# Up projections of a mixture of experts loaded in halves of 2 MB, experts in a fixed order, small pieces for the last

## The chip, the cores and the metric

The kernel runs on one core of one Trainium2 chip. The metric is the device time of one execution in microseconds. Engines: PE is TensorE, DVE is VectorE, ACT is ScalarE, POOL is GpSimd, SP is SyncE, which here issues the DMAs. PEld is PE's weight load.

## The reference

One layer of an encoder trunk for 256 tokens of 2048 channels, float32. A token-mixing sub-layer comes first: RMSNorm, modulation by `c`, an input projection, four branches with gates, an output projection and a residual. The change is in the second, the experts:

```python
pg = softmax(ht @ rg_w + rg_b); pg_top, g_idx = top_k(pg, 1)          # 1 group of 4
le = (ht @ re_w + re_b).reshape(t, 4, 8); le = le[:, g_idx]           # its 8 experts
pe_top, e_idx = top_k(softmax(le), 2); weights = pg_top * pe_top / sum(pe_top)
y[e] = (silu(x @ w1[e]) * (x @ w3[e])) @ w2[e]     # w1, w3: 2048 x 512, w2: 512 x 2048
x = x + gt2 * sum over the two experts of weights * y[e];  out = rmsnorm(x, final_g)
```

There are 32 experts, each of 12 MiB: w1 and w3 (the up projections) of 4 MiB each, w2 (the down projection) of 4 MiB.

## The kernel before

The mixing part runs until about 800 us. Its output x1 (2 x 128 tokens, in `r_h`) is split into three bfloat16 parts, `xparts`, whose sum is x1. The router sorts the 512 pairs of token and expert by expert and cuts each expert's pairs into windows of 64 (`NWIN`). Each window is a **pass**. The number of passes, `n_pass`, is 32 if no expert has more than 64 pairs, as here, and at most `MAXPASS`, 39. `etab` holds the expert of each pass, `otab` its offset, `ntab` the number of passes; SP, PE, ACT and DVE read them into registers once `table_ready` is set. A loop over 1 to 38 with a condition `p < end_p` does the middle passes; the last is written out.

One pass on PE: `gather` (line 886) multiplies columns of `xparts` (the weights of the matmul) by a 0/1 matrix, two halves of 48 matmuls. DVE's `modulated` makes `xe` of it, which is scaled and shifted. `turn` (895) transposes the hidden values of the pass before, `turn_windows` (918) its windows. `first` (954, `first_last` 979 in the last pass) is the up projection of this pass, 16 blocks of 128 channels in four chunks of four. `second` (908, `last_second` 1058) is the down projection of the pass before, `combine` (935) adds its result back into token order, and DVE's `add_moe` (1762) adds it to x1. Between them stand DVE's `window` (1733), `hidden` (1768), `save_output`, `output_low`, and ACT's `select`, `silu`, `copy_windows`, `round_output`, `copy_hidden`.

Weights lie in `ring` (slots 0 to 3, eight chunks of 1 MiB for up weights; slot 4 for half of w2) and `r_b` (the other half). SP issues all loads in one order: for pass p, chunk 0 of w1 and w3, half of w2 of the pass before, chunk 1, the other half, chunk 2, chunk 3. It waits before each for `w13_used` or `w2_used`, which PE raises at the end of a chunk. A partition reads four rows of w1, 8 KB that lie together, or two rows of w2, 16 KB:

```python
e1_v = exp_w1.rearrange("e (c p j) n -> e p c j n", c=4, p=P)
xparts_k = xparts[:, :, :, :].rearrange("p i t (c q j) -> p i t c j q", c=4, j=4)
```

So block k of `xe` holds every fourth channel, and `gather` reads its weights with 8 bytes between columns; the transposes of x1 (815) and of the modulation rows (681) read float32 with 16 bytes between columns, except the rows of the last vector of three, which are contiguous.

Ahead of the table: chunks 1 to 3 and w2 of expert 0 are issued while the output projection runs, chunk 0 into `r_m` after the logits, and chunk 0 of the next pass's expert once the table is there.

Of the kernel before, what the change touches and what calls it, by code (L numbers as in the profile page):

```python
# [18 lines left out]
P = 128  # L19
# [9 lines left out]
F = D // 4  # L29
# [41 lines left out]
N_KEEP = K_EPS + 1  # L71
# [3 lines left out]
def build(nc, x, ada_w, w_in, pool_w, pool_scale, branch_w, w_o, router_w, exp_w1, exp_w3, exp_w2, final_g,  # L75
          columns, router_b, gt1_bias, keep_consts, mix_consts, iota_const, out):
    with ExitStack() as ctx:
# [30 lines left out]
        x1_k = x1.rearrange("p t (c q j) -> p t c j q", c=4, j=4)  # L108
# [9 lines left out]
        pair_win = r_m[:, 0:256].rearrange("p (t m j) -> p t m j", t=TT, m=2)  # L118
# [15 lines left out]
        def first_chunk(m):  # L134

            return r_m[:, m * 2048:(m + 1) * 2048]
# [27 lines left out]
        xparts_k = xparts[:, :, :, :].rearrange("p i t (c q j) -> p i t c j q", c=4, j=4)  # L164
# [42 lines left out]
        ntab = sb("ntab", [1, 2], I32)  # L207
# [90 lines left out]
        w13_in = [sem(f"w13_in{i}") for i in range(CHUNKS)]  # L298
# [12 lines left out]
        first_in = [sem(f"first_in{m}") for m in range(2)]  # L311
# [32 lines left out]
        e1_v = exp_w1.rearrange("e (c p j) n -> e p c j n", c=4, p=P)  # L344
        e3_v = exp_w3.rearrange("e (c p j) n -> e p c j n", c=4, p=P)
# [38 lines left out]
        def _(sp):  # L384
# [89 lines left out]
            def load_w2(e, h):  # L474

                sp.dma_start((slot(4), r_b[:, :])[h].rearrange("p (f n) -> p f n", f=2),
                             e2_v[bass.ds(e, 1), :, 2 * h:2 * h + 2, :].rearrange("e p f n -> (e p) f n")
                             ).then_inc(w2_in[h], 16)
# [23 lines left out]
            for c in (1, 2):  # L502
                sp.wait_ge(g_used, 128 + 4 * (5 + c))
                load_w13(0, c)
            sp.wait_ge(wo_done, 8)
            load_w13(0, 3)
            sp.wait_ge(logitT_done, 2)
            for m, w in enumerate((e1_v, e3_v)):
                sp.dma_start(first_chunk(m).rearrange("p (k n) -> p k n", k=4),
                             w[0:1, :, 0, :, :].rearrange("e p j n -> (e p) j n")).then_inc(first_in[m], 16)  # L510
            sp.wait_ge(table_ready, 1)
            n_pass = sp.value_load(ntab[0:1, 0:1], min_val=NE, max_val=MAXPASS)
            second_e = sp.value_load(etab[0:1, 1:2], min_val=0, max_val=NE - 1)
            load_w13(second_e, 0)
            with sp.Fori(1, MAXPASS) as p:
                with sp.If(p < n_pass):
                    before = sp.value_load(etab[0:1, bass.ds(p - 1, 1)], min_val=0, max_val=NE - 1)
                    e = sp.value_load(etab[0:1, bass.ds(p, 1)], min_val=0, max_val=NE - 1)
                    with sp.If(p > 1):
                        sp.wait_ge(w13_used, 4 * p + 1)  # L520
                        load_w13(e, 0)
                        for c in (1, 2):
                            sp.wait_ge(w2_used, 4 * p + 2 * c)
                            load_w2(before, c - 1)
                            sp.wait_ge(w13_used, 4 * p + c + 1)
                            load_w13(e, c)
                    with sp.If(p < 2):
                        for c in (1, 2):
                            sp.wait_ge(w13_used, 4 * p + c + 1)
                            load_w13(e, c)  # L530
                    sp.wait_ge(w13_used, 4 * p + 4)
                    load_w13(e, 3)
            last_e = sp.value_load(etab[0:1, bass.ds(n_pass - 1, 1)], min_val=0, max_val=NE - 1)
# [1431 lines left out]
```

## Time and profile before

| | |
|---|---|
| time, median of 3 runs | 1783.74 us (1783.24 to 1787.66) |
| the profiled execution | 1783.57 us, of which the span is 1781.8 |
| PE busy | 1702.7 us, 96% of the span |
| DVE, ACT busy | 970.7 and 427.7 us |
| DMA | 641.95 MB, mean 360 GB/s |
| chain that ended last | PE 60%, DMA 35%, DVE 2% |
| up projections (line 954) | 1968 matmul records, 448.4 us |

Busy time of PE is modelled at its ends, so 96% doesn't say that PE is at its peak. The chain names, back from the last instruction, what released each step. The expert stage is the second half, from about 830 us. The DMA view counts packets; those under 512 B are the signals at the end of a transfer, one per DMA engine.

### The profile page before, as it was taken

How to read it: one execution, taken by the hardware profiler on the slowest of the kernel's cores; microseconds unless marked ns; L12 is line 12 of the kernel's file. 1: busy time of each engine (PE TensorE's matmuls, PEld its weight loads, DVE VectorE, ACT ScalarE, POOL GpSimd, SP SyncE). 2: the span in 40 equal slices, each digit the busy share in tenths (PEclk: the TensorE clock that was granted, in tenths of full speed). 3: DMA queues.
4: the chain of work that ended last, by engine and by line, in shares of the span. 5: the costliest groups of instructions: out<-in, count | busy, mean ns of one | idle time of the engine just before them, and what ended most of it. 6: DMA issues, size and time to landing. Idle time of an engine off the chain costs nothing.

```text
span 1781.8 us, 26191 instructions
## 1 busy us (share of the span) xinstructions
PE 1702.7 (96%) x10198; PEld 998.9 (56%) x10198; DVE 970.7 (54%) x1199; ACT 427.7 (24%) x534; POOL 0.9 (0%) x5
## 2 busy tenths in 40 slices
PE   4999999999999999999999999999999999999986
PEld 3888567777777776875444444444444444444442
DVE  5564959867778678566353443434343434343434
ACT  3001034433333233443121212121212121111111
POOL 0000000000000000000000000000000000000000
PEclk9999999999999999999999999999999999999998
DMA  9998538889879697835999999999999999999995
GB/s 369 387 385 323 189 142 336 334 311 352 331 287 361 259 367 317 308 131 211 414 423 425 423 425 423 425 423 425 424 425 424 424 424 425 423 425 424 425 424 241
DMA packets 128239, 641.95 MB, mean 360 GB/s; under 512 B 8003, under 2 KB 8131, under 8 KB 76099
## 3 DMA queue, kind: packets, MB, share of 16 engines
q1 hardware_dynamic: 127762, 639.18, 89.3%
q0 software_dynamic: 144, 1.70, 0.2%
q8 instruction: 31, 0.51, 0.1%
q10 hardware_dynamic: 290, 0.46, 0.1%
q14 instruction: 12, 0.10, 0.0%
HBM read 639.21 MB, written 2.10 MB: 360 GB/s over the span
## 4 chain that ended last, share of the span: by engine, by line
PE 60%; DMA 35%; DVE 2%; SPq 1%; issue 1%; DVEq 0%; ACT 0%
DMA ring<-in_exp_w 33%; PE ps L954 11%; PE ps L699 7%; PE ps L701 7%; PE ps L700 7%; PE ps L604 6%; PE ps L661 5%; PE ps L908 3%; PE ps L617 3%; DMA ring<-in_ada_w 2%; PE ps L772 2%; PE ps L773 2%; PE ps L774 2%; PE ps L886 1%; DVE r_m L1380 1%
## 5 line engine op out<-in xcount | busy, mean ns | idle before, releaser
L954 PE MATMUL ps<-ring 128*64 128x512 f32 x1968 | 448.4, 597 | 24.5 <-DMA ring<-in_exp_w 24.5
L954 PEld LDWEIGHTS ps<-ring 128*64 128x64 f32 x1968 | 145.9, 136 | 287.3 <-issue 287.2
L1762 DVE SCALAR_TENSOR_TENSOR r_h<-ps,stat,r_h 128x1024 f32<-128x1024 f32 x124 | 153.4, 1279 | 141.8 <-PE ps L935 141.8
L1721 DVE TENSOR_TENSOR r_c<-ps,scale 128x512 f32<-128x512 f32 x64 | 44.3, 692 | 305.4 <-PE ps L886 298.5
L700 PE MATMUL ps<-g_lo,h_hi 128*128 128x512 f32 x512 | 199.3, 389 | 0.0
L699 PE MATMUL ps<-mix_hi,h_hi 128*128 128x512 f32 x384 | 156.5, 408 | 0.0
L1155 ACT ACTIVATE mix_hi<-ring 128x1024 fp32r<-128x1024 f32 x96 | 101.5, 1061 | 222.3 <-PE ps L701 222.3
L701 PE MATMUL ps<-mix_hi,h_lo 128*128 128x512 f32 x384 | 149.6, 390 | 0.0
L1294 ACT ACTIVATE y_hi<-ring 128x512 fp32r<-128x512 f32 x62 | 38.1, 631 | 444.1 <-DVE ring L1749 444.1
L604 PE MATMUL ps<-r_h,ring 128*128 128x256 f32 x640 | 141.1, 383 | 1.3 <-ACT r_h L1106 1.3
L1472 DVE SCALAR_TENSOR_TENSOR r_m<-ring,col,r_m 128x2048 f32<-128x2048 f32 x53 | 124.4, 2347 | 31.8 <-DMA ring<-in_ada_w 31.8
L1486 DVE TENSOR_TENSOR g_lo<-ring,mix_hi 128x1024 fp32r<-128x1024 f32 x96 | 115.0, 1223 | 33.7 <-ACT mix_hi L1155 32.3
L604 PEld LDWEIGHTS ps<-r_h,ring 128*128 128x128 f32 x640 | 122.7, 192 | 18.3 <-issue 1.4
L886 PEld LDWEIGHTS ps<-r_c,xparts 128*128 128x128 bf16 x3024 | 106.0, 118 | 40.5 <-issue 39.6
L886 PE MATMUL ps<-r_c,xparts 128*128 128x64 bf16 x3024 | 112.8, 198 | 3.4 <-issue 3.4
L908 PE MATMUL ps<-r_b,r_c 128*64 128x512 f32 x496 | 113.2, 598 | 0.0
L908 PE MATMUL ps<-ring,r_c 128*64 128x512 f32 x496 | 111.7, 592 | 0.0
L700 PEld LDWEIGHTS ps<-g_lo,h_hi 128*128 128x128 f32 x512 | 96.2, 188 | 22.7 <-issue 3.6
L661 PE MATMUL ps<-ring,r_b 128*128 128x512 f32 x208 | 91.8, 592 | 0.0
L699 PEld LDWEIGHTS ps<-mix_hi,h_hi 128*128 128x128 f32 x384 | 72.2, 188 | 18.1 <-issue 2.9
L1749 DVE TENSOR_TENSOR ring<-ps,r_m 128x512 f32<-128x512 f32 x62 | 40.0, 687 | 74.8 <-PE ps L908 74.8
L701 PEld LDWEIGHTS ps<-mix_hi,h_lo 128*128 128x128 f32 x384 | 72.0, 188 | 15.2
(280 smaller groups left out, 1768.8 us busy)
## 6 DMA issues: line engine op xcount, KB each, us to landing
ring<-in_exp_w SPq DMA_DIRECT2D x254, 1024.0 KB, 23.2
ring<-in_ada_w SPq DMA_DIRECT2D x78, 1024.0 KB, 8.3
ring<-in_w_in SPq DMA_DIRECT2D x36, 2048.0 KB, 10.1
ring<-in_exp_w SPq DMA_DIRECT2D x32, 2048.0 KB, 24.3
r_b<-in_exp_w SPq DMA_DIRECT2D x32, 2048.0 KB, 25.3
ring<-in_w_in SPq DMA_DIRECT2D x20, 1024.0 KB, 14.2
r_b<-in_ada_w SPq DMA_DIRECT2D x18, 1024.0 KB, 9.9
ring<-in_w_o SPq DMA_DIRECT2D x8, 2048.0 KB, 8.3
```

Of the source, the lines that this page charges most:

```text
L604: last = mm(u[:, f, :], head_w(i)[:, kk, f * P:(f + 1) * P], hT[:, k, :], start=(begin and f % 2 == 0), stop=end, skip_group_check=True)
L661: last = mm(ps[:, y_bank(n) + t, :], lhs(k, t), rhs(k), start=(k == 0), stop=(k == kts - 1))
L699: mm(ps[:, b + t, :], h, hi[:, cols], start=(k == 0), stop=False)
L700: mm(ps[:, b + t, :], h, lo[:, cols], start=False, stop=False)
L701: last = mm(ps[:, b + t, :], h_lo[:, k, t * P:(t + 1) * P], hi[:, cols], start=False, stop=(k == KT - 1))
L886: last = mm(gat[:, kk, :], xparts_k[:, i, t, k // 4, k % 4, :], chosen[:, t, 0:NWIN], start=(t == 0 and i == 0), stop=(t == TT - 1 and i = ...
L908: last = mm(ps[side * NWIN:(side + 1) * NWIN, 4 + b, :], hid[:, f, :], chunk(CHUNKS + f)[:, q * MIX:(q + 1) * MIX], start=(f == 0), stop=( ...
L954: last = mm(ps[m * NWIN:(m + 1) * NWIN, 2, :], xe[:, k, :], w[:, kk * F:(kk + 1) * F], start=(k == 0), stop=(k == KT - 1))
L1155: A(g_hi[x % 4], slot(q % W_SLOTS)[:, (x % 4) * 1024:(x % 4 + 1) * 1024], ACT.Copy).then_inc(g_hi_done, 1)
L1472: ins = V.scalar_tensor_tensor(out=acc, in0=w, scalar=ccol[:, k:k + 1], in1=acc, op0=ALU.mult, op1=ALU.add)
L1486: V.tensor_tensor(g_lo[:, q, (x % 4) * 1024:(x % 4 + 1) * 1024], slot(q)[:, (x % 4) * 1024:(x % 4 + 1) * 1024], g_hi[x % 4].bitcast(F32), ...
L1762: V.scalar_tensor_tensor(out=x1n, in0=ps[:, (6, 4)[t]:(6, 4)[t] + 2, :].rearrange("p b n -> p (b n)"), scalar=tok_w[:, t:t + 1], in1=x1n, ...
```

## The change

- A load of up weights is 2 MiB: half of w1 or half of w3, with eight rows (16 KB) together per partition. Channel blocks are ordered 2 x 128 x 8 instead of 4 x 128 x 4, for x1, `xparts`, the modulation columns and the router's weights too. There are four pieces per pass, in four slots; `w13_used` rises twice per pass.
- SP's order is now: two pieces (the first halves), both halves of w2 of the pass before, two pieces. PE's order is first half, the whole of `second`, `gather` for the next, second half with two `combine` after its first and two after its second four blocks.
- Experts have a fixed order. Passes 0 to 15 are the first windows of experts 0 to 15, without the table. Then follow the further windows of any expert, at most 7 passes, from the table (none here), then experts 16 to 31. PE, ACT, DVE and SP each have three loops instead of one, and the condition stands only in the middle one. `ntab` gets two more entries.
- Expert 1's first piece is loaded ahead of the router, into slot 3; expert 0's last piece goes to `r_m[:, 0:4096]`.
- The last expert's second halves come in four pieces of 1 MiB, its w2 in four pieces of 1 MiB, each awaited by itself.
- DVE does both `save_output` before the next `modulated`. In the tail, the order of `last_combine` and `last_add` is by token half, `last_mean(0)` comes before the fourth add, and the squares follow that order.

```diff
+K_LATE = K_EPS + 1
+N_KEEP = K_LATE + 1
+EARLY = NE // 2
...
-        x1_k = x1.rearrange("p t (c q j) -> p t c j q", c=4, j=4)
+        x1_k = x1.rearrange("p t (c q j) -> p t c j q", c=2, j=8)
...
-        pair_win = r_m[:, 0:256].rearrange("p (t m j) -> p t m j", t=TT, m=2)
+        pair_win = r_m[:, 10048:10304].rearrange("p (t m j) -> p t m j", t=TT, m=2)
...
-        def first_chunk(m):
-
-            return r_m[:, m * 2048:(m + 1) * 2048]
+        def w13_slot(p, i):
+
+            if p == 0:
+                return r_m[:, 0:4096] if i == 3 else slot(i)
+            return slot((i + 3) % 4)
+
+        def w2_slot(h):
+
+            return slot(4) if h == 0 else r_b[:, :]
...
-        xparts_k = xparts[:, :, :, :].rearrange("p i t (c q j) -> p i t c j q", c=4, j=4)
+        xparts_k = xparts[:, :, :, :].rearrange("p i t (c q j) -> p i t c j q", c=2, j=8)
...
-        e1_v = exp_w1.rearrange("e (c p j) n -> e p c j n", c=4, p=P)
-        e3_v = exp_w3.rearrange("e (c p j) n -> e p c j n", c=4, p=P)
+        e1_v = exp_w1.rearrange("e (c p j) n -> e p c j n", c=2, p=P)
+        e3_v = exp_w3.rearrange("e (c p j) n -> e p c j n", c=2, p=P)
...
-            def load_w13(e, c):
-
-                for m, w in enumerate((e1_v, e3_v)):
-                    sp.dma_start(chunk(2 * c + m).rearrange("p (k n) -> p k n", k=4),
-                                 w[bass.ds(e, 1), :, c, :, :].rearrange("e p j n -> (e p) j n")
-                                 ).then_inc(w13_in[2 * c + m], 16)
-
+            def load_w13(p, e, i, landed):
+
+                w, c = (e1_v, e3_v)[i % 2], i // 2
+                sp.dma_start(w13_slot(p, i).rearrange("p (k n) -> p k n", k=8),
+                             w[bass.ds(e, 1), :, c, :, :].rearrange("e p j n -> (e p) j n")).then_inc(landed[i], 16)
+
+            for i in range(3):
+                sp.wait_ge(g_used, 128 + 4 * (5 + i))
+                load_w13(0, 0, i, first_in)
             sp.wait_ge(wo_done, 8)
-            load_w13(0, 3)
+            load_w13(1, 1, 0, w13_in)
             sp.wait_ge(logitT_done, 2)
+            load_w13(0, 0, 3, first_in)
+            sp.wait_ge(w13_used, 2 + 1)
+            load_w13(1, 1, 1, w13_in)
+            load_w13(1, 1, 2, w13_in)
+            sp.wait_ge(w13_used, 2 + 2)
+            load_w13(1, 1, 3, w13_in)
+
+            def load_front(p, e, prior):
+
+                sp.wait_ge(w13_used, 2 * p + 1)
+                for i in range(2):
+                    load_w13(1, e, i, w13_in)
+                for h in range(2):
+                    sp.wait_ge(w2_used, 4 * p + 2 * h + 2)
+                    load_w2(prior, h)
+                sp.wait_ge(w13_used, 2 * p + 2)
+
+            def load_pass(p, e, prior):
+
+                load_front(p, e, prior)
+                for i in range(2, 4):
+                    load_w13(1, e, i, w13_in)
+
+            with sp.Fori(2, EARLY) as p:
+                load_pass(p, p, p - 1)
             sp.wait_ge(table_ready, 1)
             n_pass = sp.value_load(ntab[0:1, 0:1], min_val=NE, max_val=MAXPASS)
+            end_p = sp.value_load(ntab[0:1, 1:2], min_val=NE - 1, max_val=MAXPASS - 1)
+            more = sp.value_load(ntab[0:1, 2:3], min_val=0, max_val=MAXPASS - NE)
+            more_end = sp.value_load(ntab[0:1, 3:4], min_val=EARLY, max_val=EARLY + MAXPASS - NE)
+            with sp.Fori(EARLY, EARLY + MAXPASS - NE) as p:
+                with sp.If(p < more_end):
+                    prior = sp.value_load(etab[0:1, bass.ds(p - 1, 1)], min_val=0, max_val=NE - 1)
                     e = sp.value_load(etab[0:1, bass.ds(p, 1)], min_val=0, max_val=NE - 1)
+                    load_pass(p, e, prior)
+            with sp.Fori(EARLY, NE - 1) as e:
+                p = e + more
+                prior = sp.value_load(etab[0:1, bass.ds(p - 1, 1)], min_val=0, max_val=NE - 1)
+                load_pass(p, e, prior)
+            load_front(end_p, NE - 1, NE - 2)
+            for j in range(2):
+                for m, w in enumerate((e1_v, e3_v)):
+                    sp.dma_start(w13_slot(1, 2 + m)[:, j * 2048:(j + 1) * 2048].rearrange("p (k n) -> p k n", k=4),
+                                 w[NE - 1, :, 1, 4 * j:4 * j + 4, :]).then_inc(last13_in[2 * j + m], 16)
+            for f in range(FT):
+                sp.wait_ge(w2_used, 4 * n_pass + f + 1)
+                sp.dma_start(chunk(CHUNKS + f), e2_v[NE - 1, :, f, :]).then_inc(last2_in[f], 16)
...
-                pe.wait_ge(x1_ready, m + 1)
+                pe.wait_ge(x1_ready, 4 * t + 2 * (n // 2) + 2)
...
+            def first_half(p, c, kks):
+
+                for kk in kks:
+                    k = 8 * c + kk
                     for m in range(2):
+                        last = mm(ps[m * NWIN:(m + 1) * NWIN, 2, :], xe[:, k, :],
+                                  w13_slot(p, 2 * c + m)[:, kk * F:(kk + 1) * F],
+                                  start=(k == 0), stop=(k == KT - 1))
+                return last
+
+            def gather_next(p):
+
+                pe.wait_ge(sel_ready, p + 2)
+                pe.wait_ge(xe_ready, 2 * p + 2)
+                gather(0, sel_e)
+
+            def first_pass():
+
+                for c in range(2):
+                    pe.wait_ge(xe_ready, c + 1)
                     for m in range(2):
+                        pe.wait_ge(first_in[2 * c + m], 16)
+                    first_half(0, c, range(8)).then_inc(w13_used, 1)
+                    if c == 0:
+                        gather_next(0)
+
+            def whole_pass(p, is_last=False):
+
+                pe.wait_ge(xe_ready, 2 * p + 1)
+                gather(1, sel_e)
+                turn(p)
+                turn_windows(p)
+                for m in range(2):
+                    pe.wait_ge(w13_in[m], 16 * p)
+                first_half(1, 0, range(8)).then_inc(w13_used, 1)
+                second(p, 0, 4)
+                if not is_last:
+                    gather_next(p)
+                pe.wait_ge(xe_ready, 2 * p + 2)
+                for m in range(2):
+                    if is_last:
+                        pe.wait_ge(last13_in[m], 16)
+                    else:
+                        pe.wait_ge(w13_in[2 + m], 16 * p)
+                first_half(1, 1, range(4))
+                for i in range(2):
+                    combine(p, i)
+                if is_last:
+                    for m in range(2):
+                        pe.wait_ge(last13_in[2 + m], 16)
+                first_half(1, 1, range(4, 8)).then_inc(w13_used, 1)
+                for i in range(2, 4):
+                    combine(p, i)
...
+            mm(ps[0:32, 1, 226:227], ones[0:32, 0:32], ct[:, 1, 0:1], start=True, stop=True).then_inc(start_done, 1)
...
+            first_pass()
+
+            with pe.Fori(1, EARLY) as p:
+                whole_pass(p)
...
+            with pe.Fori(EARLY, EARLY + MAXPASS - NE) as p:
+                with pe.If(p < more_end):
+                    whole_pass(p)
+            with pe.Fori(EARLY, NE - 1) as e:
+                whole_pass(e + more)
+            whole_pass(end_p, is_last=True)
...
-                    pe.wait_ge(w2_in[f // 2], 16 * n_pass)
+                    pe.wait_ge(last2_in[f], 16)
...
             last_combine(0, 0, 6)
+            last_combine(0, 1, 0)
             last_combine(1, 0, 2)
-            last_combine(0, 1, 0)
             pe.wait_ge(tail_added, 1)
             last_combine(1, 1, 6)
...
-            step(V.tensor_scalar(ntab[:, 1:2], ps[0:1, 1, 384:385], -1.0, None, ALU.add))
+            for i, less in ((1, 1), (2, NE), (3, NE - EARLY)):
+                step(V.tensor_scalar(ntab[:, i:i + 1], ps[0:1, 1, 384:385], -float(less), None, ALU.add))
...
+            def whole_pass(p):
+
+                off = v.value_load(otab[0:1, bass.ds(p, 1)], min_val=0, max_val=PAIRS)
+                window(p, off)
+                modulated(p, 1)
+                hidden(p)
+                for b in range(2):
+                    save_output(p, b)
+                modulated(p + 1, 0)
+                for b in range(2):
+                    output_low(p, b)
+                for i in range(4):
+                    add_moe(p, i)
+
...
-            last_add(1, 0, 2, 2)
-            last_add(0, 1, 0, 3)
-            last_add(1, 1, 6, 4)
-            v.wait_ge(fg_in, 16)
+            last_add(0, 1, 0, 2)
+            last_add(1, 0, 2, 3)
 
             def last_mean(t):
 
-                v.wait_ge(sq_done, 6 + 3 + t)
+                v.wait_ge(sq_done, 6 + 2 + 2 * t)
...
             last_mean(0)
+            last_add(1, 1, 6, 4)
+            v.wait_ge(fg_in, 16)
             scaled(0, 0)
+            scaled(0, 1)
             last_mean(1)
-            scaled(0, 1)
             scaled(1, 0)
             scaled(1, 1)
```

## Rows read from the trace of the kernel before

**Rows 1.** the page's 40 slices of the span, GB/s of the DMA engines

```profile
GB/s 369 387 385 323 189 142 336 334 311 352 331 287 361 259 367 317 308 131 211 414 423 425 423 425 423 425 423 425 424 425 424 424 424 425 423 425 424 425 424 241
```

**Rows 2.** busy time of PE, weight load, DVE, ACT, POOL, then clock, DMA share, GB/s

```profile
850.00:1700.00 850.00, 816.35 (x6218) 358.56 (x6216) 346.25 (x523) 156.33 (x235) 0.00 (x0) 1.00 1.01 423
```

**Rows 3.** the chain, expert stage: start us, us, what

```profile
1336.48 25.27 DMA ring<-in_exp_w
...
1366.15 25.26 DMA ring<-in_exp_w
```

**Rows 4.** the chain, passes 0 and 1 and two starts after them

```profile
829.68 7.02 PE ps L954 x32
...
838.41 7.02 PE ps L954 x32
...
847.92 3.58 PE ps L954 x16
851.51 3.43 PE ps L908 x16
...
858.37 1.72 PE ps L886 x48
...
863.68 3.43 PE ps L954 x16
...
871.82 0.68 PE ps L935 x4
...
876.02 3.58 PE ps L954 x16
...
904.11 3.58 PE ps L954 x16
```

**Rows 5.** DMA view of 830:842 us (40 slots), then 842:870 us

```profile
GB/s 0 0 0 0 0 273 164 55 191 437 437 410 437 437 437 437 410 437 437 437 437 437 437 219 27 27 410 27 0 246 410 437 382 437 437 410 410 437 382 437
DMA packets 481, 3.56 MB, mean 297 GB/s; under 512 B 47, under 2 KB 47, under 8 KB 47
...
DMA packets 1390, 11.25 MB, mean 402 GB/s; under 512 B 153, under 2 KB 153, under 8 KB 153
```

**Rows 6.** DMA view of 10:60 us, then 1041:1700 us

```profile
DMA packets 9729, 19.35 MB, mean 387 GB/s; under 512 B 289, under 2 KB 289, under 8 KB 9728
...
DMA packets 31978, 279.43 MB, mean 424 GB/s; under 512 B 3552, under 2 KB 3552, under 8 KB 3552
```

**Rows 7.** the chain, the last two passes

```profile
1692.47 25.27 DMA ring<-in_exp_w
...
1717.88 3.65 PE ps L954 x16
...
1722.67 3.39 issue
...
1729.51 4.14 PE ps L979 x16
...
1757.56 8.78 PE ps L1058 x32
```

**Rows 8.** busy time in five us of the tail, as rows 2

```profile
1755.00:1760.00 5.00, 3.41 (x14) 1.59 (x16) 0.42 (x1) 2.75 (x5) 0.00 (x0) 0.79 0.53 221
```

**Rows 9.** weight loads of lines 681 (two windows), 886, 852: ns min/median/max

```profile
L681 PEld LDWEIGHTS ps<-keep,r_m x16: 197/204/212, 472.6 to 482.7; 128*128 128x128 f32 x16
...
L681 PEld LDWEIGHTS ps<-keep,r_m x16: 138/139/141, 589.3 to 599.3; 128*128 128x128 f32 x16
...
L886 PEld LDWEIGHTS ps<-r_c,xparts x3024: 110/118/134, 827.9 to 1727.9; 128*128 128x128 bf16 x189
...
L852 PEld LDWEIGHTS ps<-xparts,r_c x8: 95/98/98, 813.4 to 821.7; 128*128 128x128 bf16 x8
```

**Rows 10.** the timeline, PE at line 681, strided and contiguous

```profile
472.78 0.63 PE L681 MATMUL ps<-keep,r_m 128*128 128x128 f32 x4
...
589.49 0.60 PE L681 MATMUL ps<-keep,r_m 128*128 128x128 f32 x4
```

More of the change, by code:

```diff
@@ L70 @@
 K_EPS = K_W + 3 * MAXWIN
-N_KEEP = K_EPS + 1
+K_LATE = K_EPS + 1
+N_KEEP = K_LATE + 1
+EARLY = NE // 2
 N_MIXC = 1024 * 3 + 256
@@ L937, in combine @@
                 last.then_inc(comb_done, 1)
-            def first(p, with_second):
-                for c in range(4):
-                    if c % 2 == 0:
-                        pe.wait_ge(xe_ready, 2 * p + c // 2 + 1)
+            def first_half(p, c, kks):
+                for kk in kks:
+                    k = 8 * c + kk
                     for m in range(2):
-                        if not with_second and c == 0:
-                            pe.wait_ge(first_in[m], 16)
-                        elif c == 0:
-                            pe.wait_ge(w13_in[m], 16 * p)
-                        else:
-                            pe.wait_ge(w13_in[2 * c + m], 16 * p + 16)
-                    for kk in range(4):
-                        k = 4 * c + kk
-                        for m in range(2):
-                            w = first_chunk(m) if c == 0 and not with_second else chunk(2 * c + m)
-                            last = mm(ps[m * NWIN:(m + 1) * NWIN, 2, :], xe[:, k, :], w[:, kk * F:(kk + 1) * F],
-                                      start=(k == 0), stop=(k == KT - 1))
-                    last.then_inc(w13_used, 1)
-                    if with_second and c == 0:
-                        second(p, 0, 2)
-                    if c == 1:
-                        pe.wait_ge(sel_ready, p + 2)
-                        pe.wait_ge(xe_ready, 2 * p + 2)
-                        gather(0, sel_e)
-                    if c == 1 and with_second:
-                        second(p, 2, 4)
-                    if with_second and c >= 2:
-                        for i in range(2):
-                            combine(p, 2 * (c - 2) + i)
@@ L969, in first_last @@
-            def first_last(p):
-                for c in range(4):
-                    if c % 2 == 0:
-                        pe.wait_ge(xe_ready, 2 * p + c // 2 + 1)
-                    for m in range(2):
-                        pe.wait_ge(w13_in[2 * c + m], 16 * p + (16 if c else 0))
-                    for kk in range(4):
-                        k = 4 * c + kk
-                        for m in range(2):
-                            last = mm(ps[m * NWIN:(m + 1) * NWIN, 2, :], xe[:, k, :],
-                                      chunk(2 * c + m)[:, kk * F:(kk + 1) * F],
-                                      start=(k == 0), stop=(k == KT - 1))
-                    last.then_inc(w13_used, 1)
-                    if c < 2:
-                        second(p, 2 * c, 2 * c + 2)
-                    if c == 2:
-                        for i in range(4):
-                            combine(p, i)
@@ L990, in _ @@
+            pe.sem_inc(w13_used, 2)
             pe.sem_inc(w2_used, 8)
```

148 lines of the change are left out of this document (59 added, 89 removed).

## Prediction, made before the changed kernel was run

> **What bounds the kernel now.** I read the page's slices first, then the busy time by stage, then the chain of waits, then the DMA view. The slices show 414 to 425 GB/s in all but the last slice of the expert stage, and 131 and 211 in the two before it, where the router runs [rows 1]. From 850 to 1700 us the DMA share is 1.01, while PE is busy 816 of 850 us [rows 2]: both look full, so the chain must decide. In its middle it repeats one link: 25.3 us from the issue of an expert's weights to their landing, one piece of up projection on PE, and the next issue. From issue to issue is 29.67 us [rows 3]. An expert is 12 MiB (8 of up, 4 of down projection), 12.58 MB, so 29.67 us is 424 GB/s: the queue sets the pace. PE alone is quicker: early on, while it lives on preloaded weights, one pass takes 904.11 - 876.02 = 28.09 us [rows 4]. PE thus has 1.6 us to spare per pass; the queue has nothing. Only three things can move the end: when the queue gets its bytes after the router, what a byte costs, and the PE chain behind the last landings.
>
> **The queue's start.** The line w13_used is what the loads wait for. Before: 12 MiB of expert 0 lie ready at the router, and the first 2 MiB of the next expert wait for the table. GB/s by slots of 0.3 us show data from about 832.7, a gap from 836.9 to 838.7, then data again; the piece that let the second load go ended at 829.68 + 7.02 = 836.70, so an idle queue needs 2.0 us from release to data [rows 4, 5]. In 830 to 842 and 842 to 870 us it moved 3.56 and 11.25 MB [rows 5]; taking off 13 us at 424 GB/s (5.51 MB) leaves 9.30 MB by 857.0, with the 12 MiB about 20.8 MiB.
> After: expert 1 is known without the table, so 14 MiB lie ready. Releases now come in halves. The first half of pass 0 ends at 836.70: 4 MiB flow from 838.7 to 848.5. Its second half ends at 838.41 + 7.02 = 845.43: 2 MiB, until 853.4. The next release is the first half of pass 1, now 7.0 us long from 847.92, so 854.9, data at 856.9: the queue is dry for 3.5 us. At 856.9 it has 20.0 MiB. That is 0.8 MiB or **+2.0 us** behind before: preloading gives 2 MiB, and coarse release takes back more.
> From there, does it stay full? Pass 1 by the rows: down projection of 7.0 us until 861.9, gather 1.7, then 3.6 + 1.1 + 3.5 until 871.9, data at 873.9; the queue has work until 876.5. First half of pass 2 ends 876.0 + 7.0, data at 885.0, queue until 886.3. These margins of 2.6 and 1.3 us are thin, but grow by over 1.2 us per pass. In the steady state a half is released 12.3 + 7.0 + 2.0 us after the previous landing, against a pass of over 29 us, so 6 to 8 us are spare. I cost it at nothing; without that margin it would cost what is missing, once per pass.
>
> **What a byte costs.** Up weights come in rows of 16 KiB instead of 8 (eight rows of w1 behind one another), down weights had 16 already. Two rows give the cost of a packet: at 2 KB packets the saturated queue does 9729 packets, 19.35 MB in 50 us; in the expert stage 31978 packets, 279.43 MB in 659 us [rows 6]. Without the small packets (289 and 3552) that is 16 x 50 us / 9440 = 84.7 ns per packet of 2050 B, and 16 x 659 / 28426 = 370.9 ns per 9830 B. The line through both is 0.0368 ns per byte and 9.3 ns per packet. A pass has 1280 data packets, 80 per engine; after, 768, 48 per engine: 32 x 9.3 = 0.30 us off 29.67, so 29.37. From 21 MiB to the 368 that are through with pass 30 are 28.9 passes: **-8.7 us**. Bounds: nothing, if a packet over 8 KiB costs twice, and 12 us, if the intercept were 13 ns. I take 8.7, since the mix already holds 16 KiB packets.
> The Trainium skill ("DMA: Bandwidth & Descriptors", section "Why small descriptors are slow (HBM only)") speaks of a fixed overhead of about 3 cycles per packet, and holds that packing is only worth it up to 256 B. An estimate from that page, at its 850 MHz, is 3.5 ns per packet, so 3.3 us over the stage instead of 8.7, a total near 1782.4. The rows differ from it: they give 9.3 ns.
>
> **The stretch behind the last landings.** The last up piece of pass 30 landed at 1692.47 + 25.27 = 1717.74 before [rows 7]; by the two terms it lands at 1711.0. Before, PE then does one piece of 3.7 us and combines; then all is idle for 3.39 us ("issue" [rows 7]), where the loop of up to 38 runs through eight empty iterations. Pass 31 starts at 1729.51, 11.8 us after the landing. After, the two halves' worth is larger: 863.68 to 876.02, the same work from the second-last piece on, is 12.34 us [rows 4]: **+0.6 us**, coarser by 4.5 and without 3.9 of stall. The seven empty iterations that now stand in the middle cost some 3 us on each engine at pass 16 (3.39 x 7/8); the queue's 6 us of margin cover them, and PE regains them at 1.3 us per pass. Without that cover they cost 3.
> From pass 31 on: 14.0 for half and down projection, 3.6 + 1.1 + 3.5 to the last half's end at 22.2, 4.2 to the window (871.82 to 876.02 in the rows of a pass, DVE's adds in front of it), about 1 to the hidden product, so 27.5 instead of 1757.56 - 1729.51 = 28.05 [rows 7]: **-0.5 us**. The pieces of 1 MiB land about when that ends (8 MiB behind the first half's landing, 20 us), so they don't bind. The last down projection takes 8.78 us instead of 7.0, with a granted clock of 0.79 where it begins, so part of it at 1.2 GHz, after PE had waited for the hidden product [rows 7, 8]; PE waits there after the change too, and I leave it. Four adds, four scalings and two means on DVE are reordered, not fewer: nothing, plus or minus 0.5.
>
> **What else is added.** One 1-column matmul, one DVE operation of some 0.1 us ahead of the pass table, two behind it: nothing to 0.3 us, I take nothing, since PE still has gather parts to do. Waits for two x1 chunks instead of one: DVE is ahead of the transposes there. The order of DVE's modulated and save_output: both end before the combine that waits for them.
> Every gather reads its weights from xparts with 16 bytes between columns, not 8. What rows show of strides: float32 weights took 139 ns to load when contiguous and 204 when 16 bytes apart, yet four such transposes took 0.60 and 0.63 us; bfloat16 took 98 contiguous and 118 at 8 bytes [rows 9, 10]. No row has bfloat16 at 16 bytes. Below: nothing. Above: the 65 ns of float32 in place of the 20, all exposed, 96 x 45 ns = 4.3 us per pass. I take nothing, because the float32 row with one element in 16 bytes lengthened the load by a third and the sequence by only 10 ns each.
>
> **Sum.** -8.7 + 2.0 + 0.6 - 0.5 = -6.6. The profiled execution took 1783.57 us (span 1781.8), 0.2 under the median of 1783.74; so 1777.0, a span of 1775.2, 0.37% less.
>
> **Rivals.**
> *Row length is worth little* (0.20): the packet cost is by bytes above 8 KiB, and passes stay at 29.6. For: down weights with 16 KiB already in the mix, and the total stays under 425. Against: the fit. Then 1777.0 + 8.7 = 1785.7.
> *PE becomes the bound* (0.15), the slower side: gather's weight loads at 16 bytes. A gather has 48 matmuls in 1.72 us, 36 ns each [rows 4]; if each takes twice that (the bound above is 45 more), 96 of them add 3.4 us, a pass is 31.5, and pass 31 starts at 876 + 29 x 31.5 + 3 = 1792.5, so the total is 1783.6 - 0.5 + 63.0 = 1846. It decides from passes of 29.6 us on, so from 16 ns more per matmul. The Trainium skill ("SBUF — State Buffer", the note on cachelines) wants at least two hits in a 16-byte line for full bandwidth: 8 bytes apart has two, 16 has one. The float32 rows agree in kind, by 65 ns.
> *The queue runs dry early or at pass 16* (0.07): margins of 1.3 us are missed in several passes, 3 to 8 us, 1780 to 1785 and a bit over.
> *More is won* (0.06): intercept near 13 ns, or the clock stays up in the tail, 1770 to 1774.
> The forecast itself has 0.52, by itself 1772 to 1782.
>
> **Range and chances.** 1770 to 1790 leaves out the PE-bound rival and little else. 0.3% (5.4 us) is what can be told from no change. Faster than 1778.4: four fifths of the forecast's 0.52 and the 0.06, 0.48. Within: the rest of the forecast, the row-length rival, half the dry queue, 0.34. Slower: 0.18.
>
> **What would show it.** Landing to landing in the middle: 29.4 right, 29.67 wrong for the row term; over 30 with a DMA share under 1 means PE bounds. Gather of 48 at 1.7 us right, 3 wrong. The DMA rate has a hole near 853 to 857 and none at pass 16. The stall of 3.4 before the last pass is gone, and pass 31's first matmul is near 1723.4, the last down projection 27.5 later. The prediction fails if any of the first three fails; each alone is larger than the margin to 0.3%.

## The result: slower, with TensorE full where the queue had been

The changed kernel took 1821.19 us (median of 4 runs, 1818.2 to 1824.83), the one before 1783.96 beside it on the same chip: a ratio of 1.0206, interval 1.0192 to 1.022. The forecast was 1777.0 with a range to 1790, so both the time and the sign were wrong. The profiled execution took 1820.09 us, with a span of 1818.0. One of the eleven executions of the second kernel with packed parts (below) took 3566.03 us, twice the others, and is left out of its ratio.

The same views after, the page's slices first, with GB/s in 40 slices of the span:

```profile
GB/s 370 387 373 305 185 162 351 334 291 362 335 300 319 288 361 299 301 194 140 414 421 414 418 419 415 420 413 422 399 364 423 413 423 412 422 414 423 413 421 186
```

The busy time of PE, weight load, DVE, ACT and POOL in the expert stage, then clock, DMA share and GB/s:

```profile
850.00:1700.00 850.00, 843.78 (x5988) 408.27 (x5986) 326.15 (x497) 117.09 (x198) 0.00 (x0) 0.99 0.99 411
```

And one pass of the chain (start us, us, what):

```profile
912.07 3.02 PE ps L913 x48
...
915.87 7.02 PE ps L971 x32
922.89 6.87 PE ps L935 x32
929.76 3.02 PE ps L913 x48
932.77 3.58 PE ps L971 x16
936.36 1.12 PE ps L962 x8
937.48 3.58 PE ps L971 x16
941.07 1.12 PE ps L962 x8
942.19 3.02 PE ps L913 x48
945.21 0.56 PE ps L922 x4
945.77 0.22 PE ps L945 x2
```

Before, this chain repeated one 25.3 us transfer per expert [rows 3]; now it is PE from end to end, with no transfer and no other engine in it. The next pass starts at 945.99, so a pass is 30.12 us instead of 29.67. PE went from 816 to 844 of 850 us, and the queue from 423 to 411 GB/s [rows 2]: the slices no longer stand at one level but swing, most of them between 412 and 423. Two pieces of the pass stand out: the gathers (L913, which was L886) take 3.02 us for 48 matmuls where they took 1.72 [rows 4]. Their weight loads (ns min/median/max) show why:

```profile
L913 PEld LDWEIGHTS ps<-r_c,xparts x3024: 142/166/176, 831.0 to 1765.9; 128*128 128x128 bf16 x189
```

A load takes 166 ns instead of 118 [rows 9], and a matmul of the group 63 ns instead of 36 (a 48th of its time). 96 gather matmuls per pass at 27 ns more are 2.6 us.

PE also stops once in the middle, where the loop over extra passes makes seven turns that do nothing. That is the other sizeable piece in the changed kernel's chain:

```profile
1302.51 1.12 PE ps L962 x8
1303.63 6.22 issue
1309.85 3.10 PE ps L913 x48
```

and the tail, from the first matmul of pass 31:

```profile
1766.94 7.02 PE ps L971 x32
...
1794.07 8.65 PE ps L1089 x32
```

Pass 31 starts at 1766.94, not at the predicted 1723.4. What follows it takes 51.1 us, where the forecast had 51.8. So the loss lies ahead of pass 31: 6.4 of the 43.5 us have gone by the second half of pass 0, which begins at 844.84 instead of 838.41 [rows 4], and the passes behind it add the rest.

### The profile page after: what moved, and what is told of

It is laid out like the page before. It is cut to its first block, busy times and chain, and to the rows that moved or that the text cites. A ratio compares the mean times of both kernels' runs of the same rounds, so it can differ in the third digit from the quotient of the medians.

```text
span 1818.0 us, 25263 instructions
## 1 busy us (share of the span) xinstructions
PE 1768.8 (97%) x10200; PEld 1070.2 (59%) x10200; DVE 966.9 (53%) x1202; ACT 388.0 (21%) x503; POOL 0.8 (0%) x5
## 4 chain that ended last, share of the span: by engine, by line
PE 93%; DMA 3%; DVE 2%; SPq 1%; issue 1%; ACTq 0%; DVEq 0%; ACT 0%
PE ps L971 25%; PE ps L935 12%; PE ps L913 10%; PE ps L726 6%; PE ps L728 6%; PE ps L727 6%; PE ps L631 6%; PE ps L688 5%; PE ps L962 4%; PE ps L644 3%; DMA ring<-in_ada_w 3%; PE ps L799 2%; PE ps L801 2%; PE ps L800 2%; DVE r_m L1421 1%; PE ps L922 1%
## 5 line engine op out<-in xcount | busy, mean ns | idle before, releaser
L971 PE MATMUL ps<-ring 128*64 128x512 f32 x2032 | 461.5, 598 | 0.0
L971 PEld LDWEIGHTS ps<-ring 128*64 128x64 f32 x2032 | 138.8, 137 | 257.6 <-issue 256.3
L913 PEld LDWEIGHTS ps<-r_c,xparts 128*128 128x128 bf16 x3024 | 187.7, 168 | 43.6 <-issue 42.4
L913 PE MATMUL ps<-r_c,xparts 128*128 128x64 bf16 x3024 | 194.5, 226 | 6.5 <-issue 6.2
L1314 ACT ACTIVATE r_m<-ps 128x512 f32<-128x512 f32 x32 | 19.1, 597 | 297.1 <-PE ps L971 297.1
```

Of the source, the lines that this page charges most:

```text
L913: last = mm(gat[:, kk, :], xparts_k[:, i, t, k // 8, k % 8, :], chosen[:, t, 0:NWIN], start=(t == 0 and i == 0), stop=(t == TT - 1 and i = ...
L971: last = mm(ps[m * NWIN:(m + 1) * NWIN, 2, :], xe[:, k, :], w13_slot(p, 2 * c + m)[:, kk * F:(kk + 1) * F], start=(k == 0), stop=(k == KT ...
```

## The experiments

The theory after the result: the 16 bytes between the gather's weight columns make PE the bound. The rivals: 2 MB pieces that are released late, or the new order of the waits, hold PE back; or the stall at pass 16 does it.

**The gather alone set back.** The changed kernel with the gather's view as before, so 8 bytes between columns. It takes other channels of each token than the reference; all other work is the same. Here and in the versions with other strides, the gather for the first half of pass 0 (line 1032), which is not shown, gets the same edit.

```diff
-        xparts_k = xparts[...].rearrange("p i t (c q j) -> p i t c j q", c=2, j=8)
+        xparts_k = xparts[...].rearrange("p i t (c q j) -> p i t c j q", c=4, j=4)
...
-    last = mm(gat[:, kk, :], xparts_k[:, i, t, k // 8, k % 8, :], ...
+    last = mm(gat[:, kk, :], xparts_k[:, i, t, k // 4, k % 4, :], ...
...
```

> The changed kernel, only that gather reads its weights with 8 bytes between columns as before (so it takes the wrong channels of x1 for each block; the routing doesn't depend on it). Theory 'stride': 16 bytes between bfloat16 columns made each gather matmul 63 ns instead of 36 and PE the bound. Then gathers of 48 go back to 1.7 us, PE alone needs 28.1 us or less per pass, the queue is the bound again with 29.4 us from landing to landing, and the time is 1776 to 1781. Rival 'halves': releasing weights in halves and running the whole down projection in one go makes PE or the queue wait by itself. Then the time stays above 1790 though the gathers are short. If the rows of 16 KB save nothing, passes are 29.67 and the time is 1784 to 1790.

Measured: 1781.13 us, ratio to before 0.998 (0.997 to 0.999), just over the expected 1776 to 1781. 40 us come back with this edit alone, while the late releases, the new order and the stall are all still there, so none of them makes the loss by itself. The weight loads, and the chain late in its expert stage:

```profile
L913 PEld LDWEIGHTS ps<-r_c,xparts x2592: 110/118/134, 903.5 to 1684.3; 128*128 128x128 bf16 x200
```

```profile
1665.34 20.27 DMA ring<-in_exp_w
...
1694.72 20.26 DMA ring<-in_exp_w
```

The queue is the bound again, with 29.38 us from issue to issue.

**The gather alone changed.** The kernel before, with the gather at 16 bytes and nothing else (so here too other channels).

```diff
-        xparts_k = xparts[...].rearrange("p i t (c q j) -> p i t c j q", c=4, j=4)
+        xparts_k = xparts[...].rearrange("p i t (c q j) -> p i t c j q", c=2, j=8)
...
```

> The kernel before, only that gather reads its weights with 16 bytes between columns (wrong channels again). Theory 'stride': a gather of 48 goes from 1.7 to 3.0 us, a pass on PE from 28.1 to between 30.1 and 30.7, PE becomes the bound, and the time is 1803 to 1820. Rival 'halves': stride costs little where the rest is as before, 1784 to 1788.

Measured: 1815.31 us, ratio 1.0173 (1.0156 to 1.019). Two rows of its chain, one pass apart, and the busy time, columns as above:

```profile
1363.81 3.03 PE ps L886 x48
...
1367.61 3.58 PE ps L954 x16
...
1397.74 3.58 PE ps L954 x16
```

```profile
1320.00:1690.00 370.00, 370.00 (x2623) 178.24 (x2621) 147.08 (x223) 65.54 (x98) 0.00 (x0) 1.00 1.00 418
```

30.13 us per pass, PE busy 370 of 370 us, in a kernel with old rows, old releases and its loop at the end. So the theory is shown from both sides: the stride is enough to make the slow pass, and without it the slow pass is gone.

**Contiguous weights.** One look at the changed kernel whose gather reads 256 contiguous bytes for each load (other channels).

```diff
-    last = mm(gat[:, kk, :], xparts_k[:, i, t, k // 8, k % 8, :], ...
+    last = mm(gat[:, kk, :], xparts[:, i, t, k * P:(k + 1) * P], ...
...
```

> The changed kernel, only that gather reads contiguous weights (wrong channels), with xparts written as before. If the issue of small matmuls is the floor, 48 still take 1.6 to 1.7 us; if the load sets their pace even at 8 bytes, they take 1.3 to 1.4 us. Time within 2 us of the one with 8 bytes, since the queue is the bound. Beside the packed one it shows what the strided writes cost ahead of the router.

Measured: 1780.98 us. A load takes 98 ns and 48 matmuls 1.51 us, but a pass late in the stage still takes 29.36 us, as with the 8-byte gather: once PE is under the queue's 29.4 us, more speed there is worth nothing. The equal total is in part chance. Pass 31 starts 1.25 us earlier than with 8 bytes (1726.42 against 1727.67), and then the last down projection takes 10.04 us instead of 7.09, with a granted clock of 0.50 in its first 3 us where the other trace has 1.00.

**Other strides.** Views with 32 and with 4 bytes, one look each.

```diff
-        xparts_k = xparts[...].rearrange("p i t (c q j) -> p i t c j q", c=2, j=8)
+        xparts_k = xparts[...].rearrange("p i t (c q j) -> p i t c j q", c=1, j=16)   # or c=8, j=2
...
```

> The changed kernel with the gather's weights read with 32 bytes between columns instead of 16 (it takes the wrong channels: for its time only). If the load of a strided weight grows with every doubling of the stride (98 ns contiguous, 118 at 8 bytes, 166 at 16), a matmul of the gather takes 80 to 120 ns instead of 63, 48 take 4 to 6 us, and a pass 32 to 36 us: 1870 to 2000 us. If what counts is only that each column lies in a 16-byte piece of its own, 32 bytes cost as 16 do: 3.0 us for 48, passes of 30.1 us, 1821 us.

> The changed kernel with the gather's weights read with 4 bytes between columns (it takes the wrong channels: for its time only). A load between the contiguous one and that of 8 bytes: 98 to 118 ns, 1.5 to 1.7 us for 48, queue-bound passes of 29.4 us, 1779 to 1783 us. If any stride costs as much as 8 bytes do, 118 ns and 1.72 us.

Measured: 1827.59 and 1781.78 us. The groups of weight loads from 1300 to 1700 us (busy us, mean ns | idle before them), for 32 bytes and then for 4:

```profile
L913 PEld LDWEIGHTS ps<-r_c,xparts 128*128 128x128 bf16 x1247 | 80.1, 166 | 21.6 <-issue 21.6
```

```profile
L913 PEld LDWEIGHTS ps<-r_c,xparts 128*128 128x128 bf16 x1344 | 40.8, 98 | 16.5 <-issue 16.5
```

A load at 32 bytes costs what it does at 16. Its 48 matmuls take 3.12 to 3.15 us against 3.02 and a pass 30.3 instead of 30.12, which makes up the 6 us over the changed kernel, where 1821 was expected. 4 bytes cost nothing. So the price of a load doesn't grow with the distance: it stops once each column lies in a 16-byte piece of its own. With one, two, four or eight columns to such a piece a load took 166, 118, 98 and 98 ns. The Trainium skill ("SBUF — State Buffer", section "Specifications (TRN2)", row "Cachelines") asks for two hits in such a line for full bandwidth. The runs agree that one hit is dear (166 ns); with two, a load was still 20 ns over the contiguous one.

**The length of a row.** The changed kernel with 4x128x4 ordering of all channels, as before: its transfers are still 2 MB, of 8 KB rows, and its gather has 8 bytes. Only the edit of the loads is shown.

```diff
-            e1_v = exp_w1.rearrange("e (c p j) n -> e p c j n", c=2, p=P)
+            e1_v = exp_w1.rearrange("e (c p j) n -> e p c j n", c=4, p=P)
...
-                sp.dma_start(w13_slot(p, i).rearrange("p (k n) -> p k n", k=8),
-                             w[bass.ds(e, 1), :, c, :, :].rearrange("e p j n -> (e p) j n"))
+                sp.dma_start(w13_slot(p, i).rearrange("p (c k n) -> p c k n", c=2, k=4),
+                             w[bass.ds(e, 1), :, 2 * c:2 * c + 2, :, :].rearrange("e p c j n -> (e p) c j n"))
...
```

> The changed kernel with its rows ordered 4x128x4 as before: a transfer of an up projection is still 2 MB, but of two rows of 8 KB for each partition, and the gather reads its weights with 8 bytes between columns. All else is the changed kernel's, and the computation is the reference's. If the length of a row sets the queue's rate (9.3 ns for each row fewer, as the prediction had it), a pass of the last part goes back from 29.38 to about 29.67 us and the time is 7 to 9 us over the run with 16 KB rows and an 8-byte gather (1781.1): 1788 to 1790 us. If the size of a transfer does it, passes stay at 29.4 us and the time within 2 us of that run.

Measured: 1790.38 us, ratio 1.0043 (1.0028 to 1.0058).

```profile
1647.69 7.02 PE ps L972 x32
...
1677.35 7.02 PE ps L972 x32
```

29.66 us per pass, as before the change [rows 3]. The median is 9.3 us over that of the run with 16 KB rows; by the two ratios it is 11 us. The row term was right in sign, cause and size (0.28 us per pass over 28.9 passes are 8.1 us, forecast 8.7). Note what this kernel also says: without the longer rows the other parts of the change lose 6 to 8 us.

**Packed parts, two ways.** The gather could read well if the parts of each token were stored in its order. The first try lets ScalarE write them with 256 bytes between columns; the second lets it write contiguous runs and read x1 (float32) with 32 bytes between columns, and TensorE move x1 so.

```diff
+    def parts_of(i, t, b): return xparts_p[:, i, t, b // 2, (b % 2) * 64:(b % 2 + 1) * 64, :]   # (q j): first
+    def parts_of(i, t, b): return xparts_p[:, i, t, b // 2, :, (b % 2) * 64:(b % 2 + 1) * 64]   # (j q): second
...
-    mm(ps[:, bank, :], minus, xparts[:, 0, t, b * MIX:(b + 1) * MIX], ...
+    mm(ps[:, bank, :], minus, parts_of(0, t, b), ...
...
```

> The changed kernel with xparts stored in the order in which gather reads it (128 channels of a block side by side): ACT writes the three parts with strides, and the two subtractions ahead of the router read them with strides; the output is the reference's. Theory 'stride': gather's weights load in about 98 ns, passes are bound by the queue at 29.4, and the time is that of the changed kernel with 8 bytes or up to 2 us under it, 1774 to 1781, unless the strided writes and reads cost more than 3 us once. Rival 'halves': above 1790.

> The changed kernel with the parts of the tokens stored in the order in which the gather reads them, so that each weight load reads 256 contiguous bytes; here ScalarE writes contiguous runs of 64 columns and reads x1 with a stride of 32 bytes (in the earlier run it was the write that was strided, 2.77 us for 512 columns). The computation is the reference's. If only the strided write of ScalarE and the strided moving operand of the router were dear, the gather takes 1.5 us for 48, the first up projection of pass 0 starts within 3 us of the changed kernel's, a pass of the last part takes 29.4 us, and the time is 1777 to 1784 us. If a strided read is as dear on ScalarE as a strided write, the stage in the middle is 10 to 30 us longer and the time 1790 to 1815 us.

Measured: 1815.53 us (ratio 1.0171, 1.0154 to 1.0188) and 1785.55 us (ratio 1.0011, 1.0001 to 1.002). The first missed its 1774 to 1781 by 34 us, the second lies between its two ranges. Groups from 780 us on, first kernel:

```profile
L1273 ACT ACTIVATE xparts<-ps 128x512 bf16<-128x512 f32 x8 | 19.3, 2780 | 0.0
L1268 ACT ACTIVATE xparts<-ps 128x512 bf16<-128x512 f32 x8 | 19.2, 2774 | 0.0
L1260 ACT ACTIVATE xparts<-r_h,stat 128x2048 bf16<-128x2048 f32 x2 | 18.9, 9434 | 1.2 <-DVE r_c L1638 0.6 <-DVE r_m L1638 0.6
```

and second kernel, TensorE and ScalarE:

```profile
L876 PE MATMUL ps<-r_h,r_m 128*128 128x512 f32 x8 | 8.1, 1106 | 0.0
L876 PE MATMUL ps<-r_h,r_c 128*128 128x512 f32 x8 | 8.0, 1095 | 0.0
...
L1261 ACT ACTIVATE xparts<-r_h,stat 128x2048 bf16<-128x2048 f32 x2 | 8.2, 4076 | 1.7 <-DVE r_m L1639 1.1 <-DVE r_c L1639 0.6
L1269 ACT ACTIVATE xparts<-ps 128x512 bf16<-128x512 f32 x8 | 4.8, 594 | 10.9 <-PE ps L879 10.9
```

The gather did become cheap (98 ns a load, 1.51 us for 48), and the cost moved ahead of the first pass. A scattered bfloat16 write of 512 columns took 2.77 us against 0.6; a scattered read made a matmul with a float32 moving operand (the one that streams past the weights) 1.10 us instead of 0.61, and a part 4.08 us instead of 2.00. In the first the up projection of pass 0 began at 866.08 us, 32 after the changed kernel's 834.0; in the second the chain has eight pairs of these matmuls at 1.83 to 2.01 us instead of 0.86 to 1.05, 8 us more.

**Parts in two halves.** Scattered reads that keep four numbers (16 bytes) together: channel c*1024 + 8q + 4h + l is stored at h*1024 + c*512 + 4q + l. ScalarE writes contiguous runs of 256, and the gather's columns are 8 bytes apart.

```diff
+        xparts_k = xparts[...].rearrange("p i t (h c q l) -> p i t c h l q", h=2, c=2, l=4)
+        xparts_h = xparts[...].rearrange("p i t (h n) -> p i t h n", h=2)
...
-                mm(ps[:, bank, :], root_diag[t], x1[:, t, b * MIX:(b + 1) * MIX], ...
+                mm(ps[:, bank, :], root_diag[t], x1[...].rearrange("p (n h l) -> p h n l", h=2, l=4), ...
...
-                A(xparts[:, 0, t, :], x1[:, t, :], ACT.Copy, ...
+                A(xparts_h[:, 0, t], x1[:, t, :].rearrange("p (n h l) -> p h n l", h=2, l=4), ACT.Copy, ...
...
```

> The changed kernel with each part of a token stored in two halves: channel c*1024 + 8q + 4h + l at h*1024 + c*512 + 4q + l. The gather then reads its weights with 8 bytes between columns, ScalarE reads and TensorE moves x1 in runs of four numbers (16 bytes) instead of single ones, and all stored parts are written and moved in contiguous runs of 256. The computation is the reference's. If runs of 16 bytes are read at full speed, the stage in the middle is as long as in the changed kernel (first pass within 1 us of the run with an 8-byte gather), a gather of 48 takes 1.72 us, passes of the last part take 29.38 us, and the time is 1780 to 1782.5 us, 0.1 to 0.2% under the kernel before. If the short runs cost what single numbers did (1.10 instead of 0.61 us for a moving operand, 4.08 instead of 2.00 us for a part), it is 1785 us as the run with packed weights in contiguous runs was.

Measured: 1780.09 us against 1785.27 of the kernel before on the same chip: ratio 0.997 (0.9959 to 0.998). Its groups of ScalarE and of weight loads:

```profile
L1262 ACT ACTIVATE xparts<-r_h,stat 128x2048 bf16<-128x2048 f32 x2 | 4.0, 2002 | 3.8 <-DVE r_m L1640 3.2 <-DVE r_c L1640 0.6
```

```profile
L920 PEld LDWEIGHTS ps<-r_c,xparts 128*128 128x128 bf16 x1344 | 47.0, 118 | 16.5 <-issue 16.5
```

Runs of 16 bytes are read at full speed (2002 ns, as contiguous), and the loads are back at 118 ns. Of the versions here that compute the reference for any routing, this is the only one below both kernels, by 0.3% of the kernel before.

**Without the loop in the middle.** Seven turns of it do nothing for these inputs. The loop is left out of the version in halves, and of the changed kernel; where an expert needs more windows, the result would be wrong.

```diff
-            with pe.Fori(EARLY, EARLY + MAXPASS - NE) as p:
-                with pe.If(p < more_end):
-                    whole_pass(p)
(and the same on SP, ScalarE and VectorE)
```

> The kernel with the parts in two halves and without the loop in the middle, whose seven turns do nothing for these inputs (its result is the reference's here; for inputs that need more passes it would not be). The 6.2 us in which TensorE waits for nothing at pass 16 disappear; the queue lost 1.05 us there (419 instead of 428 GB/s over 50 us), so 0.5 to 1.5 us less than the same kernel with the loop. If the wait for the queue hides it wholly, no difference; if the whole stall is on the path, 6 us less.

> The changed kernel without the loop in the middle and nothing else (its result is the reference's for these inputs). There TensorE is the bound of all passes and each microsecond that it stands counts: 6 us less than the changed kernel, 1814 to 1816 us. If the stall is hidden as in a kernel bound by the queue: 1820 to 1821 us.

Measured: 1779.95 us in halves (0.1 less than with the loop, no difference), and 1812.95 for the changed kernel (8.2 less). In the second the stall is on the path, as PE is; 6 us were expected. What is left of it there:

```profile
1304.01 0.69 issue
```

Pass 31 starts at 1760.34 instead of 1766.94. 5.5 us of that are the turns, and the pieces behind the stall, where the granted clock had been 0.83 from 1290 to 1320 us, are 1.4 shorter; 0.3 went the other way before pass 1. The rest of the 8.2 is the last down projection, 7.09 us instead of 8.65. Its first 3 us had a clock of 1.00 instead of 0.50, and no run shows that the edit did that. In the first the stall shows in the queue's rate from 1270 to 1320 us. The first of these lines is with the loop, the second without it (columns as before):

```profile
1270.00:1320.00 50.00, 42.68 (x365) 20.66 (x362) 20.54 (x28) 4.83 (x10) 0.00 (x0) 0.93 0.99 414
1270.00:1320.00 50.00, 46.74 (x380) 21.36 (x379) 23.01 (x36) 5.72 (x12) 0.00 (x0) 1.00 1.01 428
```

14 GB/s under 428 for 50 us are 1.6 us of the queue. Without the loop the last piece of pass 30 did land earlier, at 1712.71 instead of 1715.41, 0.9 of it since the passes began that much earlier. But the last down projection then took 9.82 us instead of 7.09, and the spans are both 1777.6. The granted clock in its first 3 us was 0.50 there and 1.00 in the version with the loop. Nothing in the edit touches this stretch, and two kernels that differ from the 8-byte version only in the gather's stride (contiguous and 4 bytes) had the same drop, with 10.04 and 9.92 us. So one profile hides what the loop's absence gave; whether the medians hide it too is open.

## Why the prediction was wrong

- **The failed step** is in "What else is added": of the gather's 16 bytes it says "I take nothing, because the float32 row with one element in 16 bytes lengthened the load by a third and the sequence by only 10 ns each." The term was 27 ns for each of 96 matmuls, 2.6 us per pass. The load in that row was longer by nearly half (204 ns against 139). The float32 transposes that served as evidence come four at a time. Read singly in the trace, their starts lie 108 ns apart when contiguous and 108, 119 and 122 ns with 16 bytes, so 65 ns more of load showed as 14 at most, and not at all in the first gap. Running on for 32 transposes, a version with a load of 212 ns took 3.86 us and one of 193 ns took 3.58 (lines 815 and 842): 19 ns of load, 9 per transpose. A gather matmul moves only 64 columns and takes 36 ns of its group's time with a load of 118 [rows 4, 9]; there 48 ns more of load gave 27 more per matmul, and 20 ns less (contiguous) gave 4 less. The evidence came from a short group whose own pace of 108 ns hid most of the load, and was used for a long one with a pace of 36. The rule that spoke against the change was cited and got 0.15.
- **PE's spare 1.6 us per pass** was read correctly. A pass of PE went from 28.09 to 30.12, which is 2.03 and not 2.6; the chain of a pass no longer holds VectorE's windows before the first up projection, about 0.6 us that now end beneath the longer gather. The threshold of 16 ns more per matmul left that cover out: with it, (1.6 + 0.6) us over 96 matmuls are some 23 ns, an estimate. 27 was over either. The rival "PE becomes the bound" had the mechanism and the sign, at 0.15, and took 36 ns instead of 27, so 1846 instead of 1821.
- **The row term, -8.7**, held. 29.38 us per pass was measured against 29.37 forecast, and 8 KB rows put 29.66 back. It was won only where PE left the queue to be the bound.
- **The queue's start, +2.0**, was too small. In the run with the 8-byte gather these views of the DMA from 830 to 842 and from 842 to 870 us answer to [rows 5]:

```profile
DMA packets 47, 0.77 MB, mean 64 GB/s; under 512 B 0, under 2 KB 0, under 8 KB 0
```

```profile
GB/s 445 468 421 468 398 351 445 421 445 492 421 258 234 257 374 374 398 468 398 281 117 0 0 257 94 281 351 468 374 398 421 421 468 445 445 398 421 398 492 398
```

  The hole is there (slots of 0.7 us, the 21st to 25th, 856 to 859.5 us), some 2.5 us after its forecast place, because everything from pass 0 on is late: its first half ended at 838.55 and not at 836.70, and its second half began at 840.9 and not at 838.41 [rows 4]. The second release was late too, which shows as a dip to 234 to 258 GB/s from 849.7 to 851.8 us that was not forecast. By the last landing (1714.98 instead of 1717.74, 2.8 less) the start cost -2.8 + 8.0 - 1.1 = +4.1, where 8.0 is what 28.9 passes of 29.66 us save at 428 GB/s instead of 424, and 1.1 the dip at pass 16 (419 GB/s from 1270 to 1320 us). So the mark "a hole near 853 to 857 and none at pass 16" came true late in its first part and not in its second. About 2 us of the start are the stage ahead, whose transposes (L842) began at 802.1 where they had begun at 800.1. The second kernel with packed parts, which is the same up to there, began them at 800.2, and the kernel before with only its gather changed at 802.7, so two microseconds of spread between runs are enough for it. Another 0.6 is PE's wait for ScalarE's selection (L1303) before the second gather, which was not forecast.
- **The seven empty turns** cost 6.1 to 6.2 us of PE, twice the estimate of 3. Scaling the 3.39 us of the eight turns [rows 7] was wrong; without the loop 0.69 us are left at that place, so the turns are 5.5. Why seven cost more here than eight did at the end was not tried. "The queue's 6 us of margin cover them" held but for 1.1 to 1.6 us with the queue as the bound; in the changed kernel, with no cover, they were on the path in full, with 1.4 us more for the pieces behind them at a clock of 0.83.
- **Behind the last landings, +0.6 and -0.5**: with the 8-byte gather 12.70 us from landing to pass 31 against 11.77 (+0.9), and 27.15 us to the last down projection against 28.05 (-0.9). Right within 0.4 us. The last down projection was 1.7 faster than before (7.09 instead of 8.78), which the forecast had left as it was; its first 3 us had a granted clock of 1.00 instead of 0.56.
- **Sum with the gather's term taken out**: -2.8 + 0.9 - 0.9 - 1.7 - 0.1 = -4.6 on the span (1777.2 against 1781.8), forecast -6.6; by the medians it is -3.5. Of the -4.6, 1.7 are the last down projection, which came out faster by luck. The forecast's own terms give -2.9: the row term was sound, the start cost twice its +2.0, and the item costed at nothing decided.
- **Of the marks** that were set out: the one "over 30 with a DMA share under 1 means PE bounds" and "gather of 48 ... 3 wrong" named exactly what the profile then showed (30.12 us, a share of 0.99, 3.02 us).

## What to carry to other kernels

When a layout is changed for the sake of a transfer, follow every reader of the same order through to the engine that has the least spare time, and hold its spare time (here 1.6 us of 29.7) against the widest bound of each item costed at nothing: an unmeasured 0 to 4.3 us per pass beside a margin of 1.6 is an open question and not a nothing. Take the price of a weight load from a group that is as short of cover as the one in question, since a load behind long matmuls tells little of one behind 64 columns. Here an order could be had by both sides because the reordering kept runs of 16 bytes together.

Compare the clock before two profiles are compared in the tail: in these thirteen the same 32 matmuls took 7.09 to 10.04 us, more than most of the terms that were to be told apart.

## What the runs showed of the hardware

- A bfloat16 weight load of 128x128 takes 98 ns with its columns 2 or 4 bytes apart, 118 at 8 bytes, 166 at 16 and at 32; the 64-column matmuls behind take 31, 36 and 63 ns each (a 48th of the group), and 65 to 66 at 32 bytes.
- Float32 transposes whose weight was 32 bytes apart loaded no slower than at 16 (188 to 193 ns against 204 to 212).
- ScalarE: 2.77 us for 512 bfloat16 columns written 256 bytes apart against 0.6; float32 read 32 bytes apart 4.08 us per 2048 against 2.00, and 2.00 in runs of 16 bytes.
- TensorE's moving operand: bfloat16, read 256 bytes apart, 1.02 to 1.04 us per 512 columns against 0.38, with 1.02 also where the granted clock was 1.00; float32, 32 bytes apart, 1.10 against 0.61.
- After the 6.2 us stall in the changed kernel the granted clock was 0.83 from 1290 to 1320 us, and a pair of pieces behind it took 0.91 and 0.43 us instead of 0.56 and 0.22.
- The last down projection, 32 matmuls, took 7.09 us in seven of the thirteen profiles, with a granted clock of 1.00 (2.4 GHz) in its first 3 us. It took 8.65 to 8.78 in three (0.50 to 0.56 in the first 3 us, 0.90 to 0.98 in the next 4) and 9.82 to 10.04 in three (0.50, that is 1.2 GHz, then 0.63 to 0.68). In each of them PE had been busy for 2.1 to 3.4 of the 5 us before it. So the same stretch of work was given either clock, and no run shows what decides it.
